# Keys and values of the memory made inside the expert stage, and a first attention that begins with its memory queries

## What is computed

```python
xb = x2[tok]
hb = jax.nn.silu(xb @ w_gate[e]) * (xb @ w_up[e])
return (hb @ w_down[e]) * g[:, None].astype(x2.dtype)
```

```python
km, vm = jnp.split(mem @ w_mem_kv, 2, axis=-1)
lg = jnp.einsum('bshd,bmhd->bhsm', qm, km).astype(jnp.float32) * (MEM_HEAD_DIM ** -0.5)
p = jax.nn.softmax(lg, axis=-1)
o = jnp.einsum('bhsm,bmhd->bshd', p, vm)
```

## Time and profile before

| | |
|---|---|
| runs of the kernel, 3 | median 1398.41 us (1397.78 to 1399.11) |
| the profiled execution: its own time | 1393.92 us |
| its span, first to last instruction | 1392.2 us |
| PE busy (matmuls) | 1211.5 us, 87% of the span |
| PE loading weights | 789.1 us, 57% |
| DVE / ACT / POOL busy | 468.4 / 266.8 / 320.7 us |
| moved by DMA | 335.76 MB, mean 241 GB/s |
| clock granted to PE, mean | 0.943 of full |

### The profile page before, as it was taken

How to read it: one execution, slowest core, us unless ns; L and a number is a source line. 1 busy time by engine, 2 the same in 40 slices (tenths; PEclk the granted TensorE clock), 3 DMA queues, 4 the chain that set the end, 5 groups by cost and what they waited for, 6 DMA issues and landing times.

```text
span 1392.2 us, 18472 instructions
## 1 busy us (share of the span) xinstructions
PE 1211.5 (87%) x7489; PEld 789.1 (57%) x7497; DVE 468.4 (34%) x1160; ACT 266.8 (19%) x686; POOL 320.7 (23%) x336
## 2 busy tenths in 40 slices
PE   7999998865566655668999989999999999999997
PEld 6774555321222212122777559999448665999843
DVE  3343524110101101010205655444574213544467
ACT  4313432000000000001314541111003322111100
POOL 5000100000000000000002244888200113878800
PEclk9999999978878888779999999999999999999999
DMA  9643356999999999999937018555334038555400
GB/s 343 199 164 121 121 201 259 412 428 427 429 429 428 427 428 429 426 425 415 343 121 242 1 51 281 185 181 182 137 136 152 0 112 283 194 169 182 152 1 30
DMA packets 102505, 335.76 MB, mean 241 GB/s; under 512 B 6728, under 2 KB 58240, under 8 KB 88349
## 3 DMA queue, kind: packets, MB, share of 16 engines
q1 hardware_dynamic: 99814, 326.33, 61.0%
q0 software_dynamic: 2416, 8.30, 1.7%
q10 hardware_dynamic: 199, 0.06, 0.0%
HBM read 333.59 MB, written 2.86 MB: 242 GB/s over the span
## 4 chain that ended last, share of the span: by engine, by line
PE 69%; DMA 19%; DVE 4%; POOL 3%; issue 2%; ACT 2%; SPq 1%; POOLq 0%; DVEq 0%; ACTq 0%
PE bank L1645 18%; PE bank L860 17%; DMA ring<-in_w_expert_up 17%; PE bank L1695 8%; PE bank L1215 5%; PE bank L1233 3%; PE bank L1808 2%; PE bank L1114 2%; PE bank L1619 2%; DMA ring<-in_w_expert_down 1%; PE bank L1483 1%; PE bank L1242 1%; PE bank L1031 1%; PE bank L1540 1%; PE bank L1823 1%
## 5 line engine op out<-in xcount | busy, mean ns | idle before, releaser
L860 PE MATMUL bank<-wide_rows,ring 128*128 128x256 f32 (+3 forms) x608 | 134.9, 375 | 1.9 <-DVE arena L2370 1.7
L1645 PE MATMUL bank<-R,arena 128*128 128x128 f32 x1056 | 125.1, 275 | 0.0
L1215 PE MATMUL bank<-ring,arena 128*32 128x512 f32 x512 | 73.0, 724 | 59.7 <-DMA ring<-in_w_expert_up 59.7
L860 PEld LDWEIGHTS bank<-wide_rows,ring 128*128 128x128 f32 (+1 forms) x608 | 111.7, 191 | 23.3 <-issue 6.1
L1645 PEld LDWEIGHTS bank<-R,arena 128*128 128x128 f32 x1056 | 121.5, 192 | 0.0
L1215 PE MATMUL bank<-wide_rows,arena 128*32 128x512 f32 x128 | 70.5, 704 | 54.0 <-DMA arena<-in_w_expert_up 54.0
L3087 POOL DMA_DIRECT2D wide_rows<-in_g_final x1 | 0.6, 575 | 469.5 <-PE bank L1233 469.5
L2616 DVE TENSOR_TENSOR arena<-arena,bank 64x512 f32<-64x512 f32 x16 | 11.1, 691 | 285.2 <-ACT arena L2069 285.2
L1645 PE MATMUL bank<-wide_rows,ring 128*128 128x128 f32 x704 | 91.2, 275 | 1.0 <-ACT arena L1859 0.7
L1645 PEld LDWEIGHTS bank<-wide_rows,ring 128*128 128x128 f32 x704 | 84.8, 192 | 2.2 <-ACT wide_rows L2052 1.1
L3106 POOL TENSOR_TENSOR arena<-arena,small 128x512 f32<-128x512 f32 (+1 forms) x44 | 38.1, 866 | 193.3 <-DVE small L2794 152.7
(11 more groups left out here) (367 smaller groups left out, 1950.4 us busy)
## 6 DMA issues: line engine op xcount, KB each, us to landing
ring<-in_w_expert_down SPq DMA_DIRECT2D x29, 2048.0 KB, 14.2
ring<-in_ffn_w_in SPq DMA_DIRECT2D x44, 1024.0 KB, 8.1
ring<-in_w_expert_gate SPq DMA_DIRECT2D x16, 2048.0 KB, 23.1
ring<-in_w_expert_up SPq DMA_DIRECT2D x16, 2048.0 KB, 31.9
arena<-in_w_expert_up SPq DMA_DIRECT2D x14, 2048.0 KB, 30.8
ring<-in_ffn_w_out SPq DMA_DIRECT2D x10, 2048.0 KB, 7.7
ring<-in_w_in SPq DMA_DIRECT2D x7, 2048.0 KB, 16.0
arena<-in_w_expert_gate SPq DMA_DIRECT2D x7, 2048.0 KB, 25.7
```

Source lines behind the costliest of these rows:

```text
L860: last = pe.matmul(dst, lhsT, rhs, start=k == 0, stop=k == len(pairs) - 1)
L1215: last = pe.matmul(bank[e % 2][at:at + SLOTS, :], xg_tile(e % 2, k)[:, SLOTS * r:SLOTS * r + SLOTS], w[r][:, kk, :], start=k == 0, stop=k ...
L1645: last = pe.matmul(up_banks[layer][u % 4][i][:, at * P:(at + 1) * P], weights(k), columns(k), start=k == 0, stop=k == KT // 2 - 1)
```

## The change

- **mem** (1 MB) is loaded into X, which is free during the experts, behind the units of pair 2 (counted from 0). `mem_columns` turns it in quad 1, ahead of the gate products of pair 3, through banks 2 and 3, and ACT writes it back into X.
- **w_mem_kv** of layer a in quad 1, of layer b in quad 2, is loaded into slot 0 of the experts' ring (`mem_weights`). The gate unit that used to go there for the second pair of the quad is issued after it has been read: SP issues units 1, 2, 3, waits for `mem_made`, then issues 0, 4, 5.
- **Products**: PE makes keys (side 0) and values (side 1) of a layer between the turns and the down products of the quad's first pair, into banks 2 and 3. ACT copies them to three small staging places; POOL stores them to DRAM (`by_memory`, 12 transfers, 1 MB in all); ACT waits for the store before it fills the staging places again. Quads 1 and 2 are written out, the loops begin at 3.
- **Back**: behind the last experts SP loads the a_in weights in the order 2, 1, 0, then `by_memory` in one transfer, then cmp_k, cmp_v. The slots that mem and its weights had are "free" and take feed-forward weights earlier.
- **Second block**: no memory products are left there. The x columns are followed by a_qm, computed by block of 128 tokens (`first_project_a`), and the memory steps 0 to 3 stand among the other projections. In front of the first feed-forward, pieces of `first_columns` stand where the memory products were.

```diff
@@ -109,8 +109,8 @@
-    order += [("mem", 0), ("mem_kv_a", 0), ("a_in", 0), ("a_in", 1), ("a_in", 2), ("cmp_k", 0)]
-    order += [("mem", 1), ("a_out", 0), ("cmp_v", 0), ("mem_kv_b", 0), ("a_out", 1)]
+    order += [("a_in", 0), ("a_in", 1), ("a_in", 2), ("cmp_k", 0), ("cmp_v", 0), ("free", 5)]
+    order += [("a_out", 0), ("free", 1), ("free", 2), ("a_out", 1), ("free", 4)]
...
 def first_attention():
-    return [("a_q", 0), ("a_kv", 0), ("a_q", 1), ("a_q", 2), ("a_kv", 1), ("cmp_h", 0), ("a_qm", 0), ("cmp_hT", 0), ("step", 0),
-            ("a_v", 0), ("cmp_kv", 0), ("step", 1), ("mem_a", 2), ("cmp_l", 0), ("mem_a", 3), ("step", 2), ("mem_b", 0), ("step", 3),
-            ("step", 4), ("mem_b", 1), ("step", 5), ("cmp_pT", 0), ("step", 6), ("summed", 6), ("step", 7), ("step", 8), ("summed", 7),
+    return [("a_qm", 0), ("a_kv", 0), ("step", 0), ("a_q", 0), ("step", 1), ("cmp_h", 0), ("step", 2), ("a_q", 1), ("cmp_hT", 0),
+            ("step", 3), ("a_v", 0), ("cmp_kv", 0), ("a_q", 2), ("cmp_l", 0), ("a_kv", 1), ("step", 4), ("step", 5), ("cmp_pT", 0),
+            ("step", 6), ("summed", 6), ("step", 7), ("step", 8), ("summed", 7),
...
+        memT = [X[:, k % 2, k // 2 * MEM:(k // 2 + 1) * MEM] for k in range(KT)]
...
+        mem_stage = [(0, MEM, w_router[:, :, :].rearrange("p k n -> p (k n)")[:, 0:MEM]), (MEM, P, tri[:, :]),
+                     (MEM + P, P, wide_rows[:, 0:P])]
         expanded = sem("expanded")
...
-            last_job = {("mem_kv_a", 0): ("mem_a", 3), ("mem_kv_b", 0): ("mem_b", 3), ("mem", 1): ("mem_b", 3),
+            last_job = {("free", 1): ("a_kv", 1), ("free", 2): ("a_kv", 1), ("free", 4): ("cmp_h", 0),
...
-            for c, job in ((0, ("a_q", 1)), (1, ("a_kv", 1)), (2, ("a_v", 0))):
+            for c, job in ((0, ("a_q", 1)), (1, ("a_kv", 1)), (2, ("a_kv", 1))):
...
+                elif (what, c) == ("free", 5):
+                    sp.wait_ge(moe["down"], 2 * DUOS)
...
             for u in range(SPARES, 6):
                 used_up(u, 2)
                 next_unit(u, 2, False)
+            sp.dma_start(X[:, :, :], mem_2[0].rearrange("(b p) d -> p b d", p=P)).then_inc(mem_in, 16)
+
+            def mem_weights(layer, i):
+
+                used_up(0, i * 2 + 1)
+                src = kmaj((a_w_mem_kv_2, b_w_mem_kv_2)[layer][0])
+                sp.dma_start(slot(base, src.shape[1], src.shape[2]), src).then_inc(mem_weights_in, 16)
+
+            def odd_pair(i, memory=None):
                 for u in range(6):
+                    if u == SPARES and memory is not None:
+                        mem_weights(memory, i)
                     used_up(u, i * 2 + (0 if u < SPARES else 1))
                     next_unit(u, i * 2 + 1, u < SPARES)
 
@@ -804,7 +802,12 @@
                     used_up(u, i * 2 + (1 if u < SPARES else 2))
                     next_unit(u, i * 2 + 2, False)
 
-            with sp.Fori(1, LAST_QUAD) as i:
+            for layer in range(2):
+                odd_pair(1 + layer, memory=layer)
+                even_pair(1 + layer, (1, 2, 3))
+                sp.wait_ge(mem_made, 2 * layer + 2)
+                even_pair(1 + layer, (0, 4, 5))
+            with sp.Fori(3, LAST_QUAD) as i:
                 odd_pair(i)
                 even_pair(i)
             odd_pair(LAST_QUAD)
...
             second = first_unit["second"]
-            for u in (0, 1, 2, 3, 4, 5, 8, 9, 10, 7):
+            for u in (2, 1, 0):
+                load(second + u)
+            used_up(1, DUOS)
+            sp.wait_ge(mem_stored, 16 * 3 * 4)
+            sp.dma_start(arena_and_mem[:, ARENA:ARENA + half_unit], by_memory).then_inc(mem_back, 16)
+            for u in (3, 4, 6, 9):
                 load(second + u)
...
+            def mem_columns():
+                pe.wait_ge(mem_in, 16)
+                for j in range(4):
+                    if j >= 2:
+                        pe.wait_ge(mem_kept, j - 1)
+                    for r in range(2):
+                        for tb in range(TB):
+                            last = pe.transpose(bank[2 + j % 2][:, r * T + tb * P:r * T + (tb + 1) * P],
+                                                X[:, tb, (2 * j + r) * P:(2 * j + r + 1) * P], ident[:, :])
+                    last.then_inc(mem_turned, 1)
+
+            def mem_product(layer, side):
+
+                w = ring[:, base % RING, :].rearrange("p (k n) -> p k n", n=HALF)
+                if side == 0:
+                    pe.wait_ge(mem_weights_in, 16 * (layer + 1))
+                pe.wait_ge(moe["taken"], 2 * (layer + 2) + side + 1)
+                for m in range(2):
+                    if side == 0:
+                        pairs = [(w[:, k, m * P:(m + 1) * P], memT[k]) for k in range(KT)]
+                    else:
+                        pairs = [(memT[k][:, m * P:(m + 1) * P], w[:, k, MEM:2 * MEM]) for k in range(KT)]
+                    last = product(bank[2 + side][:, m * MEM:(m + 1) * MEM], pairs)
+                last.then_inc(mem_made, 1)
 
...
+            def moe_quad(i, first=False, combined=False, memory=None):
+
+                if memory == 0:
+                    mem_columns()
                 moe_gate_up(1, 0, i, first)
                 if not combined:
                     moe_combine(0, i)
                 moe_gate_up(1, 1, i)
+                if memory == 0:
+                    pe.wait_ge(mem_kept, 4)
+                elif memory == 1:
+                    pe.wait_ge(mem_staged, 2)
                 moe_gather(1, i)
                 moe_turn(1, i)
+                if memory is not None:
+                    for side in range(2):
+                        mem_product(memory, side)
                 moe_down(1, i, first)
                 moe_gate_up(2, 0, i)
                 moe_combine(1, i)
...
-            with pe.Fori(1, LAST_QUAD) as i:
+            for layer in range(2):
+                moe_quad(1 + layer, memory=layer)
+            pe.wait_ge(mem_staged, 4)
+            with pe.Fori(3, LAST_QUAD) as i:
                 moe_quad(i)
...
-            normed_to_cols("xTa", 0)
+            keep_awake(6, jobs.bank("xTa", 2))
+            for tb in range(TB):
+                turn_block("xTa", tb, 0)
...
+            def first_project_a(tb):
+
+                b = to_fill(pe, "a_qm") if tb == 0 else bank[jobs.bank("a_qm")]
+                for r in range(2):
+                    w = a_cols(1188 + r * P, P)
+                    for k in range(KT):
+                        if (tb, r) == (0, 0) and k % 4 == 0:
+                            wait_emptied(pe, "xTa", k // 4)
+                        last = pe.matmul(b[:, r * T + tb * P:r * T + (tb + 1) * P], w(k), XT[:, k, tb * P:(tb + 1) * P], start=k == 0, stop=k == KT - 1)
+                return last
+
+            first_project_a(0)
+            wait_emptied(pe, "xTa", 2)
+            wait_emptied(pe, "xTa_last")
+            first_project_a(1).then_inc(job_done, 1)
...
-                early = 2 + layer
+                early, behind = (((0, 1), (0, 1)), ((2, 0), (3, 1), (2, 1), (3, 0))) if layer == 0 else (((0, 1, 2), (0, 1, 2)), ((3, 0), (3, 1)))
                 if layer == 0:
                     turn_block(name, 0, ahead)
-                for what, part in between(name, 0):
-                    mem_product(what, part)
                 for j in range(2):
                     wait_emptied(pe, name, j)
-                    for u in range(early):
+                    for u in early[j]:
                         first_columns(u, j)
                     if j == layer - 1:
                         turn_block(name, 1, ahead)
                 if layer == 0:
                     turn_block(name, 1, ahead)
-                for what, part in between(name, 1):
-                    mem_product(what, part)
+                    for u, j in behind[:2]:
+                        first_columns(u, j)
                 wait_emptied(pe, name, 2)
                 wait_emptied(pe, name + "_last")
-                for what, part in between(name, 1):
-                    wait_emptied(pe, what, part)
-                for u in range(early, 4):
-                    for j in range(2):
-                        first_columns(u, j)
+                for u, j in behind[2 - 2 * layer:]:
+                    first_columns(u, j)
                 for u in range(FFT):
                     up(u)
...
+            def mem_columns():
+                for j in range(4):
+                    act.wait_ge(mem_turned, j + 1)
+                    act.activation(X[:, :, j * MEM:(j + 1) * MEM], bank[2 + j % 2][:, :].rearrange("p (a t) -> p a t", t=T),
+                                   ACT.Copy).then_inc(mem_kept, 1)
+
+            def mem_out(n):
+                act.wait_ge(mem_made, n + 1)
+                if n:
+                    act.wait_ge(mem_stored, 16 * 3 * n)
+                for at, w, v in mem_stage:
+                    last = act.activation(v, bank[2 + n % 2][:, at:at + w], ACT.Copy)
+                last.then_inc(mem_staged, 1)
+
```

(12 more changed lines are left out.)

81 lines of the change are left out of this document (11 added, 70 removed).

## The result

The changed kernel took 1400.46 us (median of 18 runs, 1397.51 to 1403.53). The ratio is 1.004, with a 95% interval of 1.0028 to 1.0052: slower by 0.4%, 3.9 to 7.3 us. The forecast was 1395.8 us against 1398.41, so 0.998. The time lies in the range that I gave; the direction is the other one. The two profiled executions (1400.21 and 1393.92 us) differ by 6.3 us.

What follows compares the result with a forecast made beforehand. Experts were taken as bound by DMA, the stretch behind them by PE. Costs 13.5 + 1.3 + 7.6 less a gain of 25.0 gave -2.6 us: 1395.8 us from 1398.41, range 1387.0 to 1404.0.

Steps and rivals of the forecast that it cites:

- net gain of the second block: Behind the experts: 28.5 us from products taken off PE, less a 3.5 us wait, leaves 25.0 us gained.
- new wait for cmp_v: Second block, before cmp_h: PE arrives before the cmp_v weights land at about 695 and waits 2.7 to 4.5, taken 3.5 us.
- the low clock in one place: Start of the second block: if a_qm meets the low clock, it ends 1.8 us later, at 677.0 instead of 675.2.
- the eight products off the path: Second block: PE loses eight memory products; gains of 7.9 at the start, 14.1 in attention, 6.5 before feed-forward, together 28.5 us.
- The expert stage: Stage bound by DMA: pays 13.5 us for bytes, 1.3 for stores and 7.6 for the ring slot's holes.
- The ring slot: Quads 1 and 2: held-back unit lands 39.1 and 38.1 us after L, the first pair's last up landing; loses 4.3 and 3.3.
- The 6.8 us worked out in the prediction: Expert stage: alternative landing time for the held-back unit instead of 7.8; holes then 5.6 us together, sum 2.0 us lower.
- What I held for free: Expert stage: turns of mem and ACT's waits for stores cost nothing; PE has about 8 us of slack in each pair.
- 1 (no holes, no wait): Expert stage and second block: ring slot's holes and cmp_v wait don't open; 1384.7 to 1388.2 us; chance 0.25.
- 2 (a longer dry stage): Slot 0, quads 1 and 2: late products leave the queue empty longer; 1405.8 us from 5 us more each; chance 0.17.
- 3 (fillers needed): First attention: steps without pieces between them leave softmax open, half of 14.1 us stays; 1402.9 us; chance 0.08.
- The signs named ahead: Profile: experts 20 to 25 us later, two DMA dips, one cmp_h wait, 25 us less behind experts, no memory product after 660.

Runs made afterwards that it cites:

- experiment 2: Changed kernel with 24 products of zeros on PE ahead of the wait before cmp_h; 1398.52 us, ratio 1.0025 to the kernel before.
- experiment 7: Changed kernel, order kept, loading only half of the cmp_v weights (1 MB instead of 2); 1394.83 us, ratio 1.0000 to the kernel before.
- experiment 4: Changed kernel with keys or values of one layer made in each of quads 1 to 4; 1394.67 us, ratio 1.0012 to the kernel before.
- experiment 6: experiment 4 without the four loads of memory weights, the slot still kept back until the products end; 1392.33 us, ratio 0.9972 to the kernel before.
- experiment 1: Changed kernel with a_q1 put ahead of cmp_h and a_v between cmp_h and its transposes; 1391.28 us, ratio 0.9984 to the kernel before.
- experiment 3: Changed kernel with each memory product summed over only half of its k tiles; 1391.23 us, ratio 0.9977 to the kernel before.
- experiment 5: Changed kernel with the edits of experiment 1 and experiment 4 together; 1389.22 us, ratio 0.9956 to the kernel before.
- experiment 9: experiment 4 without memory weight loads, their ring slot or the loads' wait; products stay, on memory columns; 1384.04 us, ratio 0.9922 to the kernel before.
- experiment 8: Changed kernel with the first attention in the order of the kernel before, only memory queries first; 1403.51 us, ratio 1.0060 to the kernel before.

## Why the prediction was wrong

**The step that failed is the net gain of the second block, 25.0 us forecast and 15.7 measured.** Within it the term "new wait for cmp_v", sized 3.5 us with bounds of 2.7 to 4.5, was mis-sized (it took 6.7), and TensorE's lower clock on the work behind a wait was not in the sum at all (2.5 us on cmp_h).

- The wait was 6.7 us, 3.2 more than the 3.5 of the sum. PE came at the early end of its bounds: 30.2 us behind the start of the last expert sums (682.43, in the kernel before 660.45), where the bounds were 30.35 and 32.15 and the 3.5 us wait stands for 31.35. That is 1.1 us of the 3.2. Most of the rest is the weights, which landed 36.7 us behind that start instead of 34.9. I had argued that as many bytes are ahead of cmp_v as were ahead of cmp_k, and so took over the end of the burst. This held only roughly. The DMA view of 683 to 722 us of the changed kernel, in 40 slices:

```profile
GB/s 390 383 400 390 376 400 375 399 384 382 412 391 431 381 395 389 393 389 402 350 354 339 342 357 345 334 343 352 345 347 352 349 340 250 121 48 20 0 0 0
```

  In the earlier trace rows five of six slices before the fall are at 317 to 349; here, with two compression weights at the end of the burst and not one, fourteen are at 334 to 357. The totals from the start of the last sums to the landing close the sum, before (660.45 to 695.34 us) and changed (682.43 to 719.12):

```profile
DMA packets 6558, 12.26 MB, mean 352 GB/s; under 512 B 144, under 2 KB 4240, under 8 KB 6556
...
DMA packets 7343, 12.65 MB, mean 345 GB/s; under 512 B 155, under 2 KB 5420, under 8 KB 7212
```

  0.39 MB more are 1.1 us, and the lower rate is 0.7: together the 1.8 us between 34.9 and 36.7. About half of these bytes (an estimate from 0.5 us at 428 GB/s) is there because the last expert loads were issued 21.5 us ahead of the sums (660.90) and not 22.0 (638.44). In the other kernels that load the full cmp_v the landing is 34.7 to 36.5 us behind the sums, so my bounds were also narrower than what one order of loads gives. I had priced these weights at the rate of the others.
- The lower clock: cmp_h 2.5 us longer, a_kv 1.3, an output piece 1.6, 5.4 together. Experiments 2 and 7 bear out that cmp_h's share comes from the wait. The two later ones are not settled. In experiment 7 both vanish, but experiments 4 and 6, with waits of 5.1 and 4.9 us, also have a_kv at 7.13, and experiment 1 has it at 8.81 without any wait. I had counted the low clock in one place, a_qm at the start, and there it did not come: a_qm ended 14.7 us behind the sums, the early end of my bounds. It came there in experiments 2, 3 and 5 (a_qm 8.54, 8.27 and 8.11 us against 7.31, the turn before it 1.55, 1.81 and 1.97 against 1.09), 1.7 us each time, near the 1.8 that I had. So where the low clock falls changes with small shifts of the timeline.
- The gain itself, the eight products off the path, was right: 28.5 forecast. With the wait and the rows at the lower clock taken off, the stretch is 157.8 to 158.2 us in the changed kernel and in experiments 2, 3, 4, 6, 7 and 9, so 27.9 to 28.3 under the 186.1 of the kernel before. In the order of experiments 1 and 5 it is 158.7, with one more hole of 0.73 us in front of a piece.

**The expert stage was right in sum:** 22.4 us forecast, 22.0 measured (23.2 from the first expert sum on). The ring slot, L + 39.1 and L + 38.1 forecast, L + 39.1 and L + 38.4 measured; holes of 4.3 and 3.3, measured 4.3 and 3.6 by time and 4.5 and 3.4 by the windows. Within it two small errors cancel: the products ended 0.7 us earlier than I had them (L + 30.4, not 31.1), and from issue to landing the two gates took 8.6 and 8.7 us, not 7.8. The 6.8 us worked out in the prediction from the Trainium skill (DMA: Bandwidth & Descriptors, Anatomy of one DMA) is an estimate, and the skill gives that fit for transfers issued from GpSimd, while these go through SP's queue. It is further off still. What I held for free was not all free: experiment 9 shows some 5 us of lost transfers from PE's products alone. In the changed kernel they must lie inside the holes that I had counted, since bytes (14.7) and holes (7.9) make up 22.6 of the 23.2 us.

**Rivals.** 1 (no holes, no wait) did not happen; experiments 1, 3 and 4 each make a part of it by hand. 2 (a longer dry stage) had the right sign, with the wrong place: the holes together were 8.0 us, under its bound of 10; its sign "ACT waiting for a store" did come, 6.85 us until 396.04, where I had held such a wait for free; PE has no wait for that copy. 3 (fillers needed) is false for the order of the change, whose holes in front of steps are 0.7 us, and true for the old order (experiment 8). The case that came, a wait of twice the size with a slower clock behind it, lies beyond my bound for the wait (4.5 us) and was no rival of mine.

**The signs named ahead:** experts 20 to 25 us later, yes (22.0); DMA share under 0.9 near 330 and 400, yes (0.66 and 0.77); one wait before cmp_h, yes, of double the size; 25 us less behind the experts, no (15.7); no memory product after 660, yes. Last, the base: the profiled execution before (1393.92) was near its true median (1394.69), and the 1398.41 on which the forecast stood was not. On the scale of the profile I had said 1391.3, and 1400.2 came: 8.9 us off, of which 9.3 are the second block.

## What to carry to other kernels

A change that takes work off a path bound by TensorE also makes TensorE arrive earlier at every load that follows. Go through each of them with its landing time; a wait of a few us can cost more than its length, since the work behind it may run at half the clock. Putting one independent product in front of the late load was worth 7.8 us here (known to some 2.6), the whole loss of 5.6 or more.

Side work in a stage bound by DMA is priced by three things: its bytes, the time for which its buffer is out of the rotation, and what TensorE's extra work does to the release of the others. Small pieces spread over more rounds (experiment 4) did away with the second, not with the third: 14.7 and 4.9 us were left.

An experiment that drops a load must drop what its buffer holds up too, or one hole replaces another (experiments 6 and 9).

## What was unexpected of the hardware

- The price of a wait is not smooth. The value compression product took 9.63, 9.85, 8.83 and 8.51 us behind waits of 6.7, 6.1, 5.1 and 4.9 us, 7.09 behind 3.4 us, but 10.01 behind 3.1 us (experiment 3). So the length of the wait alone does not set the clock behind it. The stretch with the 6.7 us wait was 9.2 us longer than the one with 3.4.
- An issue can hold up its queue for long. The SP queue's timeline from 660 to 720 us of the changed kernel:

```profile
662.70 18.56 SPq L705 DMA_DIRECT2D ring<-in_a_w_in  x3
681.37 5.92 SPq L845 DMA_DIRECT2D arena<-by_memory  x1
687.33 0.55 SPq L705 DMA_DIRECT2D ring<-in_a_cmp_w_k  x1
687.92 18.59 SPq L705 DMA_DIRECT2D ring<-in_a_cmp_w_v  x1
```

  The issue of cmp_v alone took 18.59 us, and its weights landed 31.2 us after its start; an issue of as many bytes, the expert gate at 326.28 with an empty queue, took 0.33. What stands ahead in the queue matters: two expert downs issued right behind the first memory weights took 13.19 us (changed kernel, 279.54), and without these weights 0.81 (experiment 9, 279.43). Whether it is the short rows of what stands ahead was not tested by itself.
- The key and value compression weights came at 334 to 357 GB/s, the attention weights ahead of them at 375 to 431, the expert weights at 428.
